# First modulation of a fused two-block network in two column halves, with the first input-projection units between them

## The chip, the cores and the metric

The kernel runs on one core of a Trainium2 chip (trn2). The metric is the device time of one execution in microseconds (us), lower is better. Before the change it is 989.19 us, the median of 3 runs from 987.23 to 992.52.

## The reference

Two transformer-like blocks on 256 tokens of width 1024, all in float32. What matters here is how the first one begins:

```python
silu_c = jax.nn.silu(c)
silu_cc = jax.nn.silu(c_ctx)
mod_l = jnp.split((silu_c @ ada_w[i] + ada_b[i])[:, None, :], 6, axis=-1)
h_l = modulate(rmsnorm(x, mix_norm_g[i]), mod_l[0], mod_l[1])      # h * (1 + scale) + shift
mod_c = jnp.split((silu_cc @ ada_w[i] + ada_b[i])[None, None, :], 6, axis=-1)
h_c = modulate(rmsnorm(xc, mix_norm_g[i]), mod_c[0], mod_c[1])
q_l, k_l, v_l, f_l = split_proj(h_l @ w_in)                        # w_in: 1024 x 2560
q_c, k_c, v_c, f_c = split_proj(h_c @ w_in)
...
```

Then come attention, a Fourier mixer, an output projection, gated feed-forward layers, a long convolution, a recurrent layer and a second attention, each a product of the 256 tokens with weights of 1024 rows or more.

## The kernel before, in words

Five engines run programs written out by hand, and wait for each other on counting semaphores. SP (the sync engine) loads the big weights, in **units** of 1 MB (128 partitions x 2048 floats, two transfers of 512 KB each) into a ring of six landing buffers `w_land`. For float32 accuracy each unit is split in two: ScalarE (ACT) writes the upper part `w_hi` (`split_hi`, L667), VectorE (DVE) writes the rest `w_lo` (`split_lo`, L1203). Both rings have three buffers. The activations are split the same way (`xT_hi`, `xT_lo`), and TensorE (PE) makes three matmuls for each product (`three`, L1950). One call of `half` (L1959) multiplies one unit with the 256 tokens: 2 token tiles x 4 row blocks x 3 matmuls of 128x512, so 24 matmuls. The two units of a 512-column chunk are its upper and its lower 512 rows; `unit_wait(u)` waits for `s_lo` (w_lo of unit u is written), and `s_used` says that a unit's buffers are free.

Ahead of unit 0 stand eight more megabytes through the same ring, which `load_unit` numbers u = -8 to -1: the columns of `ada_w` that give the first shift and scale. The first four are shift, the last four scale, each 256 rows x 1024 columns. PE multiplies them with the two condition vectors (L2060 to L2068, here called **products**, four 32-column matmuls each, 8 records in the trace), ACT copies the sums to SBUF (`ada_rows`, L791 and L793), PE adds the groups and turns them to columns (`ada0_sums`, L2054), DVE adds the bias (`mcol`, L1378) and makes the factor `a_col` (L1256, and `b_col` for the context, L1382). Only then can the tokens be scaled: x is normed (`xn`, L1252), transposed by PE (`turn_norm`, L1979), and for each of the eight row blocks DVE writes `xfull` (L1275), ACT `xT_hi` (L712) and DVE `xT_lo` (L1265).

After that, on DVE in this order: w_lo of unit 1 and 2, the statistics and norm of the context (L1248, L1252), w_lo of unit 3, the small lambda terms, `take(0)` (rotation of the first chunk's result, L1442 to L1446), w_lo of unit 4, `full_lo` for the context (`ctx_full`, L1275 and `ctxT_lo`, L1265), w_lo of unit 5, `take(1)`. On PE: chunk 0 (units 0, 1), the four small products of the Fourier matrices (L2134), the transposes of the context, chunk 1 (units 2, 3), then a wait for the last `ctx_full`, `turn_heads(0)` (transposes of the rotated result, L2096), chunk 2 (units 4, 5), `turn_heads(1)`, then chunk 2 for the context. ACT writes w_hi of a unit where its program says so; w_hi of unit 5 stands behind the eight `ctxT_hi`.

SP issues its loads in program order too, and each waits until its landing buffer is free. ACT issues small loads (rows of biases, constants), and its program goes on only when they are issued.

## Time and profile before

| what | value |
|---|---|
| median of 3 runs | 989.19 us (987.23 to 992.52) |
| the profiled execution, its own time | 991.08 us |
| span of its trace | 989.4 us |
| PE busy | 915.5 us (93%) |
| DVE busy | 740.9 us (75%) |
| ACT busy | 467.8 us (47%) |
| data moved by DMA | 229.09 MB, mean 232 GB/s |

The page of the profile gives the busy time of each engine over the span, then the span in 40 slices, the DMA queues, and the chain of work that ended last. Times inside the trace are counted from the span's start; the profiled execution's own time lies 1.7 us above its span. A row of the trace names line, engine, operation, and output and inputs; what stands in brackets is how long the engine was idle before it, and what released it. PEld is TensorE's weight load, ACTq and SPq are issues of DMAs.

### The profile page before, as it was taken

To read this page: it belongs to the slowest core of one execution; us is meant where nothing else is said; L and a number is where in the kernel's file an instruction comes from. 1 tells how busy PE (TensorE), PEld (TensorE's weight loads), DVE (VectorE), ACT (ScalarE), POOL (GpSimd) and SP (SyncE) were. 2 spreads that over 40 slices of the span, in tenths; PEclk is the share of its full clock that TensorE was granted. 3 is DMA by queue.
4 is the path that set the end of the run, shared out by engine and by line. 5 is a ranking of instruction groups with operands and counts; after the bars stand their busy time and mean duration, and the time that the engine had idled before them with its cause. 6 is when DMAs were issued, how large, how long until landed. Compare 5 with 4: busy or idle time off the path is not lost.

```text
span 989.4 us, 12483 instructions
## 1 busy us (share of the span) xinstructions
PE 915.5 (93%) x4323; PEld 718.3 (73%) x4323; DVE 740.9 (75%) x1074; ACT 467.8 (47%) x777; POOL 136.1 (14%) x204
## 2 busy tenths in 40 slices
PE   3799999899999999899978999999978998999995
PEld 0588766677888888677656688888867786777884
DVE  0598787788777768669687787677687788877574
ACT  1542247555434443453166443444336775645661
POOL 0001120404100121031001500020001020011000
PEclk8799999899999999989999999999999999999999
DMA  9987662358998888637533698898865546595001
GB/s 352 374 299 256 237 235 88 123 170 268 382 339 279 311 318 300 210 133 255 192 129 127 210 359 310 285 339 300 288 217 192 164 156 201 203 364 202 31 22 42
DMA packets 119046, 229.09 MB, mean 232 GB/s; under 512 B 8650, under 2 KB 64684, under 8 KB 119002
## 3 DMA queue, kind: packets, MB, share of 16 engines
q1 hardware_dynamic: 92608, 141.57, 41.5%
q0 software_dynamic: 24224, 86.32, 25.2%
q10 hardware_dynamic: 2170, 0.64, 0.3%
q8 instruction: 24, 0.39, 0.2%
q14 instruction: 20, 0.16, 0.0%
HBM read 227.43 MB, written 1.08 MB: 231 GB/s over the span
## 4 chain that ended last, share of the span: by engine, by line
PE 75%; DVE 13%; ACT 5%; issue 4%; DMA 2%; POOL 1%; SPq 0%; ACTq 0%; POOLq 0%; DVEq 0%
PE bank L1952 21%; PE bank L1954 20%; PE bank L1953 20%; DVE w_lo L1208 2%; DMA w_land<-ev_w_in_dram 2%; PE bank L2484 1%; DVE x L1290 1%; DVE w_lo L1321 1%; DVE tmp L1289 1%; PE bank L2325 1%; PE bank L2174 1%; PE bank L2032 1%; ACT w_hi L675 1%; DVE xT_lo L1334 1%; DMA ident<-k_ident_dram 1%
## 5 line engine op out<-in xcount | busy, mean ns | idle before, releaser
L1952 PE MATMUL bank<-w_hi,xT_hi 128*128 128x512 f32 x800 | 324.4, 406 | 21.1 <-DVE xT_lo L1334 10.3
L1954 PE MATMUL bank<-w_hi,xT_lo 128*128 128x512 f32 x800 | 314.8, 394 | 0.0
L1953 PE MATMUL bank<-w_lo,xT_hi 128*128 128x512 f32 x800 | 314.7, 393 | 0.0
L1208 DVE TENSOR_TENSOR w_lo<-w_land,w_hi 128x2048 fp32r<-128x2048 f32 x110 | 251.9, 2295 | 74.0 <-ACT w_hi L675 73.7
L675 ACT ACTIVATE w_hi<-w_land 128x2048 fp32r<-128x2048 f32 x110 | 210.3, 1915 | 117.5 <-PE bank L1954 115.1
L1952 PEld LDWEIGHTS bank<-w_hi,xT_hi 128*128 128x128 f32 x800 | 152.2, 190 | 64.1 <-issue 22.7
L1954 PEld LDWEIGHTS bank<-w_hi,xT_lo 128*128 128x128 f32 x800 | 152.0, 190 | 33.0
L1953 PEld LDWEIGHTS bank<-w_lo,xT_hi 128*128 128x128 f32 x800 | 152.4, 191 | 28.9
L1225 DVE SCALAR_TENSOR_TENSOR job_sum<-a_land,silu_c,job_sum 128x1024 f32<-128x1024 f32 x126 | 163.4, 1297 | 10.0 <-DMA a_land<-mod_w_dram 4.6
L1952 PE MATMUL bank<-w_hi,hT_hi 128*128 128x512 f32 x176 | 69.9, 397 | 2.8 <-DVE hT_lo L1579 2.8
L1954 PE MATMUL bank<-w_hi,hT_lo 128*128 128x512 f32 x176 | 68.7, 390 | 0.0
L1953 PE MATMUL bank<-w_lo,hT_hi 128*128 128x512 f32 x176 | 68.5, 389 | 0.0
L504 POOL DMA_DIRECT2D a_land<-ada_w_dram x40 | 29.3, 734 | 256.5 <-DVE job_sum L1225 256.5
L940 ACT ACTIVATE silu_g<-bank 128x256 f32<-128x256 f32 x44 | 14.5, 381 | 76.1 <-PE bank L1954 76.1
L944 ACT ACTIVATE hT_hi<-bank 128x512 fp32r<-128x512 f32 x22 | 13.2, 599 | 68.1 <-PE bank L2325 68.1
L1952 PEld LDWEIGHTS bank<-w_hi,hT_hi 128*128 128x128 f32 x176 | 33.0, 188 | 13.8 <-issue 7.3
L1954 PEld LDWEIGHTS bank<-w_hi,hT_lo 128*128 128x128 f32 x176 | 33.0, 188 | 7.1
L1953 PEld LDWEIGHTS bank<-w_lo,hT_hi 128*128 128x128 f32 x176 | 33.1, 188 | 6.5
L504 POOL DMA_DIRECT2D a_land<-mod_w_dram x24 | 17.3, 719 | 147.7 <-DVE job_sum L1225 141.9
L705 ACT ACTIVATE sq_half<-x 128x512 f32<-128x512 f32 x24 | 15.1, 630 | 44.1 <-DVE x L1290 44.1
L1575 DVE TENSOR_TENSOR hid<-silu_g,bank 128x256 f32<-128x256 f32 x44 | 16.5, 417 | 23.4 <-ACT silu_g L940 23.4
L1321 DVE TENSOR_TENSOR w_lo<-w_land,w_hi 128x1024 fp32r<-128x1024 f32 x28 | 33.7, 1217 | 0.4 <-ACT w_hi L720 0.4
(325 smaller groups left out, 1121.4 us busy)
## 6 DMA issues: line engine op xcount, KB each, us to landing
w_land<-ffn_w_dram SPq DMA_DIRECT2D x132, 512.0 KB, 5.7
a_land<-ada_w_dram POOLq DMA_DIRECT2D x40, 1024.0 KB, 6.0
a_land<-mod_w_dram POOLq DMA_DIRECT2D x24, 1024.0 KB, 5.6
w_land<-od_pw_w_dram SPq DMA_DIRECT2D x24, 512.0 KB, 4.9
w_land<-ev_w_in_dram SPq DMA_DIRECT2D x20, 512.0 KB, 11.8
w_land<-ada_w_dram SPq DMA_DIRECT2D x16, 512.0 KB, 11.3
a_land<-kv_mod_w_dram POOLq DMA_DIRECT2D x8, 1024.0 KB, 6.6
w_land<-rg_w_in_dram SPq DMA_DIRECT2D x16, 512.0 KB, 5.0
```

The source lines that it names most:

```text
L504: pool.dma_start(a_land[j % 2][:, :].rearrange("p (k n) -> p k n", k=2), kview(w)[:, 2 * j:2 * j + 2, bass.ds(col, D)]).then_inc(a_landed[ ...
L675: act.activation(w_hi[u % N_SPLIT][:, :], w_land[n % N_LAND][:, :], ACT.Copy).then_inc(s_hi, 1)
L705: act.activation(sq_half[:, n % 2, :], x[:, t, 512 * c:512 * c + 512], ACT.Square, accum_out=ss[:, 2 * t + c:2 * t + c + 1]).then_inc(sem( ...
L940: act.activation(silu_g[:, t, :], bank[t][:, 0:256], ACT.Silu).then_inc(sem("silu_g"), 1)
L944: act.activation(hT_hi[:, :, :].rearrange("p k s -> p (k s)"), bank[6][:, :], ACT.Copy).then_inc(sem("hT_hi"), 1)
L1208: dve.tensor_tensor(w_lo[u % N_SPLIT][:, :], w_land[n % N_LAND][:, :], w_hi[u % N_SPLIT][:, :].bitcast(F32), ALU.subtract).then_inc(s_lo, 1)
L1225: ins = dve.scalar_tensor_tensor(out=job_sum[:, :], in0=w, scalar=silu_c[:, c, n:n + 1], in1=job_sum[:, :], op0=ALU.mult, op1=ALU.add)
L1321: return dve.tensor_tensor(w_lo[u % N_SPLIT][:, cols], w_land[n % N_LAND][:, cols], w_hi[u % N_SPLIT][:, cols].bitcast(F32), ALU.subtract)
L1575: dve.tensor_tensor(hid[:, t, :], silu_g[:, t, :], bank[t][:, 256:512], ALU.mult).then_inc(sem("hid"), 1)
L1952: pe.matmul(dst, hi, whi, start=start, stop=False)
L1953: pe.matmul(dst, hi, wlo, start=False, stop=False)
L1954: return pe.matmul(dst, lo, whi, start=False, stop=stop)
```

## The change

The first modulation is computed in two halves of its columns: first columns 0 to 511 of shift and of scale (four units of both, `ada_half(a, 0)`), then columns 512 to 1023. SP loads the first half, x, then unit 0 and unit 2 of the old numbering (the upper 512 rows of chunks 0 and 1), then the second half, and then the rest. The new unit order is chunk 0 upper, chunk 1 upper, chunk 0 lower, chunk 1 lower (units 0, 1, 2, 3). Upper rows need only the first half of the modulation. Units 0 and 2 are split and multiplied in quarters (`x_chunk`, `x_quarter`). On PE the products of the second half stand between the matmuls of unit 1, and `turn_heads(0)` moves behind the first unit of chunk 2.

```diff
+def landing(u):
+    return u + ADA0 // 2 if u < 2 else u + ADA0
...
-HALVED = [BASE["out"] + 5, BASE["ffn0"] + 2, BASE["pw1"] + 1, BASE["pw1"] + 2, BASE["pw2"] + 5, BASE["ffn1"] + 2, BASE["rg_in"] + 1, BASE["rg_in"] + 2,
+HALVED = [0, 2, BASE["out"] + 5, BASE["ffn0"] + 2, BASE["pw1"] + 1, BASE["pw1"] + 2, BASE["pw2"] + 5, BASE["ffn1"] + 2, BASE["rg_in"] + 1, BASE["rg_in"] + 2,
...
+            def ada_half(a, h):
+                def parts(land):
+                    v = land[:, :].rearrange("p (k g n) -> p k g n", k=2, g=2)
+                    return [(v[:, :, g, :], kview(ada[0])[:, 2 * a:2 * a + 2, bass.ds(g * D + 512 * h, 512)]) for g in range(2)]
+                return parts
+            for a in range(4):
+                load_item(a, ada_half(a, 0))
             sp.dma_start(x[:, :, :], t_in["x"][0].rearrange("(t p) d -> p t d", p=P)).then_inc(sem("x_in"), 16)
+            for c in range(2):
+                load_unit(c, in_cols[c](0))
+            for a in range(4):
+                load_item(6 + a, ada_half(a, 1))
```

In ScalarE's program:

```diff
             load_rows(2)
             act.dma_start(rope[:, :, :, :], t_in["k_rope"].rearrange("(t p) c d -> p t c d", p=P)).then_inc(sem("rope_in"), 16)
+            act.wait_ge(sem("ada0_used"), ADA0 // 2)
+            act.activation(ada_rows[:, 0, :], bank[0][:, :], ACT.Copy).then_inc(sem("ada0_rows"), 1)
             act.wait_ge(sem("x_in"), 16)
             norm_square("n_x", x, xn)
...
+            split_halves(0)
+            x_hi(range(4))
+            split_hi(1)
             act.wait_ge(sem("ada0_used"), ADA0)
-            act.activation(ada_rows[:, 1, :], bank[1][:, :], ACT.Copy).then_inc(sem("ada0_rows"), 1)
-            split_hi(0)
-            split_hi(1)
-            full_hi("n_x", xfull, xT_hi)
+            act.activation(ada_rows[:, 1, :], bank[4][:, :], ACT.Copy).then_inc(sem("ada0_rows"), 1)
+            act.wait_ge(sem("four_gmm"), 1)
+            act.activation(four_g[:, :, :, :].rearrange("p c f n -> p (c f n)"), bank[4][:, :], ACT.Copy).then_inc(sem("four_gs"), 1)
+            split_halves(2)
+            x_hi(range(4, KT))
```

In VectorE's:

```diff
+            def x_quarter(k, u):
+                x_full(k)
+                x_full(k + 1)
+                split_lo_half(u, 0, half_ready(u)).then_inc(sem("w_lo_half"), 1)
+                x_low(k)
+                x_low(k + 1)
+                split_lo_half(u, 1, (s_hi, u + 1)).then_inc(s_lo, 1)
+                x_full(k + 2)
+                x_full(k + 3)
+                x_low(k + 2)
+                x_low(k + 3)
+            ada0_half(0, bank[2])
+            rows_turned(1, bank[5])
             norm_stats("n_x", x, xn)
-            rows_turned(1, bank[5])
...
+            scale_half(0)
+            x_quarter(0, 0)
             split_lo(1)
+            ada0_half(1, bank[5])
+            scale_half(1)
+            x_quarter(4, 2)
...
-            split_lo(2)
+            lambda_dots()
             norm_stats("n_ctx", ctx_x, ctx_x)
             split_lo(3)
-            lambda_dots()
             take(0)
             split_lo(4)
```

In TensorE's:

```diff
+            for a in range(4):
+                ada0_products(a)
+            ada0_sums(0, bank[2])
+            turn_rows(1, bank[5])
+            pe.wait_ge(sem("cols_in"), 2)
+            turn_norm("n_x", xn, bank[4:8])
+            def x_chunk(n, u, j):
+                pe.wait_ge(sem("w_lo_half"), n)
+                half(u, j, xT_hi, xT_lo, bank[0:2], None, "n_x", range(NT), (0, 1))
+                unit_wait(u)
+                half(u, j, xT_hi, xT_lo, bank[0:2], s_used, "n_x", range(NT), (2, 3))
+            x_chunk(1, 0, 0)
+            pe.wait_ge(*seen("full", "n_x", 4))
+            ada0_products(4)
+            pe.wait_ge(sem("ada0_cols"), 2)
+            unit_wait(1)
+            half(1, 0, xT_hi, xT_lo, bank[2:4], None, None, (0,))
+            ada0_products(5)
+            half(1, 0, xT_hi, xT_lo, bank[2:4], s_used, None, (1,))
+            ada0_products(6)
+            ada0_products(7)
+            pe.wait_ge(sem("ada0_rows"), 2)
+            ada0_sums(1, bank[5])
...
+            x_chunk(2, 2, 1)
+            pe.wait_ge(sem("four_gs"), 1)
+            pe.wait_ge(sem("cols_in"), 3)
+            turn_norm("n_ctx", ctx_x, bank[4:8])
+            unit_wait(3)
+            half(3, 1, xT_hi, xT_lo, bank[2:4], s_used)
...
+                        if (c, side, j) == (2, 0, 1):
+                            pe.wait_ge(*seen("full", "n_ctx", KT))
+                            turn_heads(0)
```

On PE, between the first matmuls of the input projection and the ones of the lower rows, the program before has nothing of the modulation; it is all ahead of unit 0 (buffer numbers: w_land_49 to 54 are the six landing buffers, w_hi_55 to 57 and w_lo_58 to 60 the two rings of three):

```order
L2066 MATMUL bank<-w_land_49,silu_pad 32x512 [waits w_landed0]
L2066 MATMUL bank<-w_land_49,silu_pad 32x512 x3
L2066 MATMUL bank<-w_land_50,silu_pad 32x512 [waits w_landed1]
L2066 MATMUL bank<-w_land_50,silu_pad 32x512 x3
L2056 MATMUL bank<-ada_sel,ada_rows 128x4 [waits ada0_rows,ada_sel]
L2056 MATMUL bank<-ada_sel,ada_rows 128x4 x3
L2056 MATMUL bank<-ada_sel,ada_rows 128x4 [waits ada0_rows]
L2056 MATMUL bank<-ada_sel,ada_rows 128x4 x3
L1952 MATMUL bank<-w_hi_55,xT_hi 128x512 [waits lo,w_lo,ada0_rows]
```

In the changed program the same engine has, from the last matmul of unit 1 to the first one of unit 2:

```order
L2021 MATMUL bank<-w_hi_56,xT_lo 128x512
L2134 MATMUL bank<-w_land_51,silu_pad 32x512 [waits w_landed2]
L2134 MATMUL bank<-w_land_51,silu_pad 32x512 x3
L2134 MATMUL bank<-w_land_52,silu_pad 32x512 [waits w_landed3]
L2134 MATMUL bank<-w_land_52,silu_pad 32x512 x3
L2123 MATMUL bank<-ada_sel,ada_rows 128x4 [waits ada0_rows]
L2123 MATMUL bank<-ada_sel,ada_rows 128x4 x3
L2117 MATMUL bank<-ident,prow 128x97 [waits prow2,ada0_cols]
L2172 MATMUL bank<-four_w,four_c 128x128 [waits consts_in]
L2172 MATMUL bank<-four_w,four_c 128x128 x3
L2019 MATMUL bank<-w_hi_57,xT_hi 128x512 [waits lo,w_lo_half]
```

So two of the products, the second sums and the Fourier products now stand between unit 1 and unit 2. ACT before, from the two copies of the sums on:

```order
L791 ACTIVATE ada_rows<-bank 128x512 [waits ada0_used]
L793 ACTIVATE ada_rows<-bank 128x512 [waits ada0_used]
L675 ACTIVATE w_hi_55<-w_land_51 128x2048 [waits w_landed2]
L675 ACTIVATE w_hi_56<-w_land_52 128x2048 [waits w_landed3]
L712 ACTIVATE xT_hi<-xfull 128x256 [waits full] x8
L675 ACTIVATE w_hi_57<-w_land_53 128x2048 [waits w_landed4]
L693 ACTIVATE ctx_junk,ss<-ctx_x 128x1024 [waits rstd,ctx_in]
L693 ACTIVATE ctx_junk,ss<-ctx_x 128x1024
```

ACT in the changed program, from the splits of unit 0 on:

```order
L743 ACTIVATE w_hi_55<-w_land_53 128x1024 [waits w_landed4] x2
L820 ACTIVATE xT_hi<-xfull 128x256 [waits full] x4
L697 ACTIVATE w_hi_56<-w_land_54 128x2048 [waits w_landed5]
L826 ACTIVATE ada_rows<-bank 128x512 [waits ada0_used]
L828 ACTIVATE four_g<-bank 128x512 [waits four_gmm]
L743 ACTIVATE w_hi_57<-w_land_53 128x1024 [waits w_landed4] x2
L820 ACTIVATE xT_hi<-xfull 128x256 [waits full] x4
L715 ACTIVATE ctx_junk,ss<-ctx_x 128x1024 [waits rstd,ctx_in]
L715 ACTIVATE ctx_junk,ss<-ctx_x 128x1024
```

The second copy of the sums and the copy of the Fourier product stand in the middle, and the split of unit 2 and the squares of the context are behind both. On PE, before `turn_heads(0)` stood between unit 3 and unit 4:

```order
L1954 MATMUL bank<-w_hi_55,xT_lo 128x512
L2096 MATMUL bank<-ident,rot 128x128 [waits rot,full]
L2096 MATMUL bank<-ident,rot 128x128 x3
L2096 MATMUL bank<-ident,rot 128x128 [waits rot]
L2096 MATMUL bank<-ident,rot 128x128 x3
L1952 MATMUL bank<-w_hi_56,xT_hi 128x512 [waits w_lo,rot]
```

Now it stands between unit 4 and unit 5:

```order
L2021 MATMUL bank<-w_hi_56,xT_lo 128x512
L2198 MATMUL bank<-ident,rot 128x128 [waits rot,full]
L2198 MATMUL bank<-ident,rot 128x128 x3
L2198 MATMUL bank<-ident,rot 128x128 [waits rot]
L2198 MATMUL bank<-ident,rot 128x128 x3
L2019 MATMUL bank<-w_hi_57,xT_hi 128x512 [waits w_lo]
```

The wait for the last `ctx_full` moves with it, from ahead of unit 4 to ahead of unit 5.

## Rows read from the trace of the kernel before

**Rows 1.** Chain of work that ended last, 15 to 90 us: start, duration, what.

```profile
39.02 0.46 DVE xfull L1275
39.48 0.33 DVE xT_lo L1265
...
49.63 1.42 DVE ctx_x L1252 x2
...
53.99 0.61 DVE rope_cos L1442
...
58.35 2.20 DVE w_lo L1208
60.55 0.47 DVE ctx_full L1275
...
66.37 1.09 PE bank L2096 x8
```

**Rows 2.** Timeline of ACT: start, duration, engine, line, operation, [idle before, releaser].

```profile
22.04 0.45 ACTq L789 DMA_DIRECT2D lam_in<-ev_lambda_k_dram  x1
...
31.31 0.60 ACT L793 ACTIVATE ada_rows<-bank 128x512 f32<-128x512 f32 x1 [8.18 <-PE bank L2066]
...
36.24 1.91 ACT L675 ACTIVATE w_hi<-w_land 128x2048 fp32r<-128x2048 f32 x1 [0.97 <-DMA w_land<-ev_w_in_dram]
...
45.58 1.04 ACT L693 ACTIVATE ctx_junk<-ctx_x 128x1024 f32<-128x1024 f32 x1
```

**Rows 3.** Timeline of DVE, the norm of x.

```profile
20.78 1.42 DVE L1252 TENSOR_SCALAR xn<-x,rstd 128x1024 f32<-128x1024 f32 x2 [0.89 <-POOL rstd L485]
```

**Rows 4.** Timeline of TensorE, 10 to 79 us: the pieces that the change moves.

```profile
10.69 5.91 PE L2066 MATMUL bank<-w_land,silu_pad 128*32 128x512 f32 x32 [0.74 <-ACT silu_pad L777]
20.45 1.94 PE L2066 MATMUL bank<-w_land,silu_pad 128*32 128x512 f32 x8 [3.85 <-DMA w_land<-ada_w_dram]
...
25.99 3.40 PE L1984 MATMUL bank<-ident,xn 128*128 128x128 f32 x16 [0.38 <-DVE pcol L1363]
29.32 1.92 PE L2066 MATMUL bank<-w_land,silu_pad 128*32 128x512 f32 x16
31.18 1.95 PE L2056 MATMUL bank<-ada_sel,ada_rows 128*128 128x4 f32 x16
39.17 0.76 PE L1952 MATMUL bank<-w_hi,xT_hi 128*128 128x512 f32 x1 [6.04 <-DVE xT_lo L1265]
...
52.24 1.08 PE L2134 MATMUL bank<-four_w,four_c 128*128 128x128 f32 x8
...
78.23 0.60 PE L2096 MATMUL bank<-ident,rot 128*128 128x128 f32 x4
```

**Rows 5.** Timeline of TensorE: matmuls at either clock, and two later pauses.

```profile
41.01 0.63 PE L1953 MATMUL bank<-w_lo,xT_hi 128*128 128x512 f32 x1
41.44 0.63 PE L1954 MATMUL bank<-w_hi,xT_lo 128*128 128x512 f32 x1
...
43.60 0.40 PE L1952 MATMUL bank<-w_hi,xT_hi 128*128 128x512 f32 x1
43.83 0.39 PE L1953 MATMUL bank<-w_lo,xT_hi 128*128 128x512 f32 x1
...
187.09 2.79 PE L2228 MATMUL bank<-ident,o_tok 128*128 128x128 f32 x12 [3.85 <-DVE o_tok L1530]
...
511.43 0.47 PE L1952 MATMUL bank<-w_hi,xT_hi 128*128 128x512 f32 x1 [3.17 <-DVE xT_lo L1746]
```

**Rows 6.** Stretches (us): busy us and instructions of PE, PEld, DVE, ACT, POOL; granted clock, DMA share, GB/s.

```profile
42.00:43.00 1.00, 1.00 (x5) 0.80 (x4) 1.00 (x4) 0.63 (x2) 0.00 (x0) 0.69 1.09 363
192.00:193.00 1.00, 1.00 (x5) 0.80 (x4) 0.85 (x4) 0.55 (x2) 1.00 (x3) 0.59 0.83 266
5.00:10.00 5.00, 0.47 (x1) 0.18 (x1) 0.18 (x2) 1.28 (x1) 0.00 (x0) 1.00 1.04 403
50.00:60.00 10.00, 10.00 (x59) 8.62 (x57) 9.79 (x19) 2.40 (x2) 1.26 (x2) 1.00 1.04 396
```

More of the change, by code:

```diff
@@ L1205, in split_lo @@
                     return
-                n = u + ADA0
+                n = landing(u)
                 dve.wait_ge(s_hi, at(u + 1, i, 6))
@@ L1380, in _ @@
[L1380 to L1385 removed]
+            bias0 = pcol[:, 0:2 * KT].rearrange("p (v h b) -> p v h b", v=2, h=2)
@@ new lines, in x_full, with x_low @@
+            def x_full(k):
+                dve.wait_ge(*seen("tr", "n_x", 4 * (k // 2) + 4))
+                dve.tensor_scalar(xfull[:, k, :], bank[4 + k // 2][:, 256 * (k % 2):256 * (k % 2) + 256], a_col[:, k:k + 1],
+                                  mc(0, k, 1), ALU.mult, ALU.add).then_inc(sem("full"), 1)
+            def x_low(k):
+                dve.wait_ge(*seen("hi", "n_x", k + 1))
+                dve.tensor_tensor(xT_lo[:, k, :], xfull[:, k, :], xT_hi[:, k, :].bitcast(F32), ALU.subtract).then_inc(sem("lo"), 1)
@@ new lines, in ada0_products @@
+            def ada0_products(a):
+                n = a if a < 4 else a + 2
+                pe.wait_ge(landed[n % N_LAND], 32 * (n // N_LAND + 1))
+                w = w_land[n % N_LAND][:, :].rearrange("p (k g n) -> p k g n", k=2, g=2)
+                for e in range(2):
+                    for g in range(2):
+                        r = 32 * (2 * e + g)
+                        ins = pe.matmul(bank[a // 4 * 4][r:r + 32, :], silu_pad[:, 2 * (a % 4) + e, :], w[:, e, g, :],
+                                        start=a % 4 == 0, stop=a % 4 == 3)
+                ins.then_inc(sem("ada0_used"), 1)
@@ new lines, in _ @@
+            turn_rows(2, bank[5])
+            pe.wait_ge(sem("consts_in"), 144)
+            for m in range(2):
+                for f in range(2):
+                    ins = pe.matmul(bank[4][:, 256 * m + P * f:256 * m + P * f + P], four_c[:, m, :], four_w[:, f, :],
+                                    start=True, stop=True)
+            ins.then_inc(sem("four_gmm"), 1)
+            x_chunk(2, 2, 1)
+            pe.wait_ge(sem("four_gs"), 1)
+            pe.wait_ge(sem("cols_in"), 3)
+            turn_norm("n_ctx", ctx_x, bank[4:8])
```

121 lines of the change are left out of this document (48 added, 73 removed).

## The prediction, as it was put on record

> **What bounds the kernel now.** I read the shares first, then the chain of work that ended last, then the timelines of the engines up to 80 us, because the change ends there. Over the whole span TensorE is busy 93% of the time, so what can be won lies where it waits. The largest such place is ahead of the first real matmul, which starts at 39.17 us after a pause of 6.04 us [rows 4]. One would think that an earlier first matmul is an earlier end. The chain says otherwise. From the landing of unit 1, which ScalarE takes up at 36.24 us [rows 2], the chain runs through VectorE: xfull and xT_lo in turn, w_lo, the norm of the context, w_lo, the rotation, w_lo, ctx_full, and only at 66.37 us does it pass to TensorE, with `turn_heads(0)` [rows 1]. TensorE meanwhile worked, but it then had to wait for the last ctx_full. Between 50 and 60 us VectorE is busy 9.79 of 10 us [rows 6]. So up to 66 us VectorE sets the time, and after it TensorE, which reaches `turn_heads(1)` at 78.23 us [rows 4]. That start is my station: behind it both programs do the same work in the same order, VectorE has slack, and what is won or lost there I carry to the end.
>
> **The change part by part, as new times of the same stations.**
>
> *First columns and x.* The products of the first half read the first four units, as before, and end at 10.69 + 5.91 = 16.60 [rows 4]. Their copy (0.60 [rows 2]) is over before x is used. The norm of x still ends at 20.78 + 1.42 = 22.20 [rows 3], since x stands in the same place of the queue. TensorE is at 1.2 GHz by then, as the 16 transposes at 25.99 were (3.40 us, 0.21 each [rows 4]); four of them give the first two row blocks at 23.2.
>
> *Unit 0.* It takes the place of the load that TensorE took up at 20.45 [rows 4], so it is there. ScalarE has issued its small loads only at 22.04 + 0.45 = 22.5 [rows 2], then splits it in two halves of 0.96 (half of 1.91 [rows 2]), to 23.45 and 24.4. VectorE: two xfull at 0.46 from 23.2 to 24.1, half a w_lo at 1.2 (half of 2.20, with its own start) to 25.3, xT_lo 0.34 to 25.7 [rows 1]. **TensorE starts the projection at about 25.9, 13.3 us earlier.** Then the two engines alternate: second xT_lo 26.0, second half of w_lo 27.2, two xfull 28.1, ScalarE's xT_hi 28.5, w_hi of unit 1 (1.91) 30.4, its w_lo (2.20) 32.6. TensorE needs 24 x 0.23 = 5.45 us for unit 0 at 2.4 GHz (0.23 from start to start at 43.60, 0.43 at 41.01 [rows 5]) and has finished with it and one product by 32.5. So unit 1 begins at 32.7, and that is VectorE and ScalarE again.
>
> *The second half of the columns.* Unit 1 costs 5.45 us, and the three products that TensorE does in and behind it 3 x 0.96 (1.92 for two at 29.32 [rows 4]), which ends at 41.0. Before, they lay in time in which it waited for data; now they lie on the path to the second columns. The last of these loads is where unit 1 was, at 36.2 [rows 2], 3.8 us before it is needed. Then copy 0.60, sums 0.98 (half of 1.95 [rows 4]), columns 0.3: 42.9, against 31.18 + 1.95 = 33.1 for all columns before. The bias transpose and Fourier products (0.2 + 1.08 [rows 4]) end at 44.2, ScalarE's copy of them at 44.8.
>
> *The rest of x.* ScalarE's halves of unit 2 stand behind that copy: 45.8 and 46.7. VectorE: half w_lo 47.0, two xT_lo 48.0, half w_lo 49.1, two xfull 50.0; ScalarE's last xT_hi 50.4. Its squares of the context, 2 x 1.04 [rows 2], are behind these: 52.5. TensorE waits from 44.2 to 47.1 and finishes unit 2 by about 55; nobody waits for that.
>
> *The old chain, later.* Statistics and GpSimd's root, 1.0 (0.89 of it the pause ahead of the norm of x [rows 3]), give 53.5, the norm 1.42 54.9 (before it ended at 49.63 + 1.42 = 51.05: **3.8 us later**), w_lo of unit 3 57.1, the rotation 58.35 - 53.99 = 4.4 to 61.5, w_lo of unit 4 63.7, ctx_full 66.33 - 60.55 = 5.8 to 69.5 [rows 1]. The lambda terms (0.8) now lie in the wait for the squares. Here the move of `turn_heads(0)` pays: unit 4 is already done. But unit 5 is not ready: its w_hi stands behind the eight ctxT_hi. 69.9, w_hi 71.8, w_lo 74.0. Its 24 matmuls end at 79.6 at full clock. **That is 1.4 us after 78.23.**
>
> *The clock.* Between the heads, over at 70.6, and unit 5 at 74.1 TensorE has nothing to do for 3.5 us. After a pause of 3.17 us a matmul took 0.47 us, its time at 2.4 GHz; after pauses of 3.85 and 6.04 us the next work ran at 1.2 GHz (transposes of 2.79 us for twelve, a first matmul of 0.76) [rows 5, 4]. The clock rose again 3.5 us after the start at 39.17 and 5.7 us after the one at 187.09: in the microseconds from 42 and from 192 it is granted 0.69 and 0.59 on the mean, so 0.5 for the first 0.6 and 0.8 of each [rows 6]. My 3.5 us lie between the two lengths, nearer to neither by much. I take the slow clock, for it fell in two of three pauses: 3.4 / 0.43 = 8 matmuls at 0.2 more, 1.6 us (2.6 at the longer rise, 0 if it stays high). The Trainium skill (TensorE: Matmul & The Clock Gate, "What's actually happening") says that the throttled state is the default and that activity releases the throttle; by that rule the idle stretch costs the 1.6 us and the median would be 992.2, by the row after 3.17 us it would cost nothing and be 990.6. The same for unit 0 costs little: if the clock rises t us after 25.9, unit 0 and a product end at 32.4 + 0.47 t, against 32.7, so 0 to 2.4 us for t up to 5.7. I take 0, since the transposes from 22.3 on are work too, and behind such transposes, which ran from 25.99, two products at 29.32 took the 1.92 us that one took before [rows 4].
>
> *Loads.* The halves are rows of 2 KB where the columns had 4 KB. Units of 2 KB rows moved 396 GB/s from 50 to 60 us, the 4 KB rows 403 from 5 to 10 [rows 6], so I cost it at nothing; unit 2 now waits for w_lo of unit 0 (27.2), with the queue filled until 36.2. In landing order it comes at about 39, the context at 42, unit 3 at 44.5, unit 4 at 47, all ahead of their use. Cover of the last product load: 3.8 us; beyond that each us costs one.
>
> **Sum:** +1.4 + 1.6 = **+3.0 us**. Against the profiled execution: span 989.4 to 992.4, its own 991.08 to 994.1. The median of the runs shown is 1.9 below that execution; 989.19 + 3.0 = **992.2 us**. The measurement tells about 0.5% (4.9 us) from no change, so this is no change that can be told, with a sign.
>
> **The rivals.**
>
> *TensorE is what bounds, and the early start comes through.* Then from 25.9 there are six units (32.7), four products (3.8), sums, Fourier products, the transposes of the context (half of 3.40) and heads (1.0 + 1.3 + 1.7 + 1.1): 67.5, 10.7 us earlier, 978.5. For it: the 6.04 us pause. Against it: behind the second columns (42.9) VectorE has 25.7 us of work of its own up to w_lo of unit 5 (a_col 0.5, half of x 3.2, unit 2 2.4, norm 1.5, lambda 0.8, three w_lo 6.6, rotation 4.4, context 6.3); even without a single wait that ends at 68.6 and unit 5 at 74.1, 4.1 us earlier, 985.1. More than 4.9 needs the second columns earlier too. 7%. Some of the waits being shorter than mine gives 0 to -4: 15%, still no change.
>
> *The slow clock decides* (the other side). If TensorE stays at 1.2 GHz through unit 0, unit 0 ends at 25.9 + 24 x 0.43 = 36.2, the product at twice its time at 38.1, and unit 1 starts 5.4 us late: 8.4 us slower, 997.6; through unit 1 also, 24 x 0.2 and 3 x 0.96 more, 16.1 us, 1005.3. For it: ahead of unit 0 TensorE has only transposes, then it waits at each pair of row blocks. Against: the products at 29.32 at the full clock, with little but transposes ahead of them. It passes the 4.9 us when the rise comes over 4.7 us after the start of unit 0 (0.47 t - 0.3 = 1.9) while unit 5 starts slow. 18%; a product load that lands over 5 us late has the same end, 3%.
>
> **How the numbers follow.** The worked chain, +1 to +4.9: 57%. Shorter waits, -4.9 to +1: 15%. Together no change within 0.5%: 72%. Faster 7%, slower 21%. The range takes the chain with the clock high at unit 5 and half of the shorter waits (-2.7, 986.5) and the chain with both longer rises (1.4 + 2.4 + 2.6 = 6.4), and 2 us, by which runs shown lie from their median: 997.5.
>
> **What would show each step.** First matmul of unit 0 near 25.9; w_lo of unit 1 over at 32.6; second mcol at 42.9; norm of the context over at 54.9; last ctx_full at 69.5 and w_lo of unit 5 at 74; second heads at 79.6 or 81.2, and the granted clock from 74 to 78. A second mcol before 40 or heads(1) before 76 would make the VectorE chain wrong; a granted clock of 0.5 beyond 31 would make the slow rival right.

## The result, and the profile after

The changed kernel takes 997.23 us (median of 7 runs, 996.36 to 999.34); the kernel before took 991.34 us in runs beside it (7 runs, 987.23 to 992.52). The ratio is 1.0062, with a 95% interval of 1.0038 to 1.0086: slower by 0.6%, a little beyond what I had called no change. The profiled executions have spans of 995.4 and 989.4 us, so +6.0 us where +3.0 was forecast.

The shares of the page say little: PE 92%, DVE 75% and ACT 47% of the span, as before within a point, and the same 229.09 MB. What changed stands in the timelines. TensorE's timeline of the changed kernel, 22 to 86 us (start, duration, engine, line, operation, idle before and releaser), against [rows 4]:

```profile
22.89 3.65 PE L2051 MATMUL bank<-ident,xn 128*128 128x128 f32 x16 [4.56 <-DVE xn L1285]
26.70 0.77 PE L2019 MATMUL bank<-w_hi,xT_hi 128*128 128x512 f32 x1 [0.16 <-DVE xT_lo L1431]
...
33.98 0.50 PE L2019 MATMUL bank<-w_hi,xT_hi 128*128 128x512 f32 x1
...
36.93 1.06 PE L2134 MATMUL bank<-w_land,silu_pad 128*32 128x512 f32 x8
...
40.88 1.93 PE L2134 MATMUL bank<-w_land,silu_pad 128*32 128x512 f32 x16
43.52 1.05 PE L2123 MATMUL bank<-ada_sel,ada_rows 128*128 128x4 f32 x8 [0.72 <-ACT ada_rows L826]
...
45.05 1.87 PE L2172 MATMUL bank<-four_w,four_c 128*128 128x128 f32 x8
50.35 0.77 PE L2019 MATMUL bank<-w_hi,xT_hi 128*128 128x512 f32 x1 [3.43 <-DVE xT_lo L1431]
...
66.46 0.47 PE L2019 MATMUL bank<-w_hi,xT_hi 128*128 128x512 f32 x1 [0.86 <-DVE w_lo L1241]
...
72.14 1.09 PE L2198 MATMUL bank<-ident,rot 128*128 128x128 f32 x8
76.71 0.80 PE L2019 MATMUL bank<-w_hi,xT_hi 128*128 128x512 f32 x1 [3.48 <-DVE w_lo L1241]
...
85.08 0.60 PE L2198 MATMUL bank<-ident,rot 128*128 128x128 f32 x4
```

The one pause of 6.04 us ahead of unit 0 is gone; the first matmul starts at 26.70 instead of 39.17. In its place stand two pauses, of 3.43 us ahead of unit 2 and of 3.48 us ahead of unit 5, and behind both the clock is low. The second heads (the start of `turn_heads(1)`) come at 85.08, 6.85 us later than before. VectorE's timeline of the same execution:

```profile
21.33 1.42 DVE L1285 TENSOR_SCALAR xn<-x,rstd 128x1024 f32<-128x1024 f32 x2 [0.90 <-POOL rstd L507]
...
44.61 0.17 DVE L1410 TENSOR_TENSOR mcol<-bank,pcol 128x8 f32<-128x8 f32 x1 [11.09 <-PE bank L2123]
...
48.53 1.23 DVE L1354 TENSOR_TENSOR w_lo<-w_land,w_hi 128x1024 fp32r<-128x1024 f32 x1 [2.25 <-ACT w_hi L743]
...
56.13 1.41 DVE L1285 TENSOR_SCALAR ctx_x<-ctx_x,rstd 128x1024 f32<-128x1024 f32 x2 [0.82 <-POOL rstd L507]
...
74.37 2.29 DVE L1241 TENSOR_TENSOR w_lo<-w_land,w_hi 128x2048 fp32r<-128x2048 f32 x1 [1.38 <-ACT w_hi L697]
```

VectorE, which had no pause left to give from 50 to 60 us, now stands idle for 11.09 us until the second sums arrive, and its whole list of later work begins behind that: the norm of the context ends at 57.54 instead of 51.05. So 6.5 of the 6.85 us stand already there. ScalarE's timeline, against [rows 2]:

```profile
42.87 0.60 ACT L826 ACTIVATE ada_rows<-bank 128x512 f32<-128x512 f32 x1 [11.68 <-PE bank L2134]
46.95 0.60 ACT L828 ACTIVATE four_g<-bank 128x512 f32<-128x512 f32 x1 [3.49 <-PE bank L2172]
47.45 1.99 ACT L743 ACTIVATE w_hi<-w_land 128x1024 fp32r<-128x1024 f32 x2
```

The split of unit 2, which needs nothing but its load, waits behind the copy of the Fourier products. The stretches give the clock (busy us and instructions of PE, PEld, DVE, ACT, POOL; granted clock, DMA share, GB/s), in order unit 0, Fourier products, unit 5:

```profile
27.00:28.00 1.00, 1.00 (x3) 0.81 (x3) 1.00 (x2) 0.00 (x0) 0.00 (x0) 0.50 0.88 283
30.00:31.00 1.00, 1.00 (x6) 0.84 (x5) 0.00 (x0) 1.00 (x1) 0.00 (x0) 1.00 1.03 398
...
45.00:47.00 2.00, 1.92 (x9) 1.62 (x9) 1.21 (x4) 0.05 (x1) 0.00 (x0) 0.54 1.05 387
76.00:82.00 6.00, 5.29 (x12) 4.13 (x13) 5.83 (x14) 2.71 (x4) 0.00 (x0) 0.50 0.53 175
```

### The profile page after: what moved, and what is told of

Its sections match the earlier page's. It is cut to its first block, busy times and chain, and to the rows that moved or that the text cites. A ratio compares the mean times of both kernels' runs of the same rounds, so it can differ in the third digit from the quotient of the medians.

```text
span 995.4 us, 12497 instructions
## 1 busy us (share of the span) xinstructions
PE 919.0 (92%) x4323; PEld 719.8 (72%) x4323; DVE 741.9 (75%) x1080; ACT 467.4 (47%) x779; POOL 136.1 (14%) x204
## 2 busy tenths in 40 slices
DMA packets 121094, 229.09 MB, mean 230 GB/s; under 512 B 8650, under 2 KB 64684, under 8 KB 121050
## 3 DMA queue, kind: packets, MB, share of 16 engines
HBM read 227.43 MB, written 1.08 MB: 230 GB/s over the span
## 4 chain that ended last, share of the span: by engine, by line
PE 75%; DVE 13%; ACT 5%; issue 4%; DMA 1%; POOL 1%; SPq 0%; POOLq 0%; ACTq 0%; DVEq 0%
PE bank L2019 21%; PE bank L2021 20%; PE bank L2020 20%; DVE w_lo L1241 2%; DVE w_lo L1354 1%; PE bank L2576 1%; DMA x<-x_dram 1%; DVE x L1323 1%; DVE tmp L1322 1%; PE bank L2417 1%; PE bank L2266 1%; PE bank L2099 1%; ACT w_hi L697 1%; PE bank L2241 1%; DVE xT_lo L1367 1%
## 5 line engine op out<-in xcount | busy, mean ns | idle before, releaser
L1241 DVE TENSOR_TENSOR w_lo<-w_land,w_hi 128x2048 fp32r<-128x2048 f32 x108 | 247.2, 2295 | 74.3 <-ACT w_hi L697 74.1
L697 ACT ACTIVATE w_hi<-w_land 128x2048 fp32r<-128x2048 f32 x108 | 206.4, 1915 | 111.7 <-PE bank L2021 111.7
L1354 DVE TENSOR_TENSOR w_lo<-w_land,w_hi 128x1024 fp32r<-128x1024 f32 x32 | 38.6, 1218 | 2.7 <-ACT w_hi L743 2.7
L743 ACT ACTIVATE w_hi<-w_land 128x1024 fp32r<-128x1024 f32 x32 | 32.4, 1049 | 3.5 <-issue 2.9
## 6 DMA issues: line engine op xcount, KB each, us to landing
w_land<-ev_w_in_dram SPq DMA_DIRECT2D x20, 512.0 KB, 10.7
```

Source lines behind the costliest of these rows:

```text
L697: act.activation(w_hi[u % N_SPLIT][:, :], w_land[n % N_LAND][:, :], ACT.Copy).then_inc(s_hi, 1)
L743: act.activation(w_hi[u % N_SPLIT][:, cols], w_land[n % N_LAND][:, cols], ACT.Copy).then_inc((sem("w_hi_half"), s_hi)[h], 1)
L1241: dve.tensor_tensor(w_lo[u % N_SPLIT][:, :], w_land[n % N_LAND][:, :], w_hi[u % N_SPLIT][:, :].bitcast(F32), ALU.subtract).then_inc(s_lo, 1)
L1354: return dve.tensor_tensor(w_lo[u % N_SPLIT][:, cols], w_land[n % N_LAND][:, cols], w_hi[u % N_SPLIT][:, cols].bitcast(F32), ALU.subtract)
```

## The experiments

"After" is the changed kernel, "station" the start of the second heads: 78.23 us before, 85.08 after. The first four ran beside one set of runs of the kernel before, then four, two and two beside others; each ratio is against its own set, whose medians lie between 989.02 and 990.58 us. Runs 1 to 3, 5, 6 and 8 have 10 executions each, run 4 has 4, run 7 has 6, runs 9 to 12 have 12.

**1. What the low clock at unit 5 costs.** Twelve matmuls whose result is thrown away fill the pause ahead of unit 5.

```diff
                             turn_heads(0)
+                            for _ in range(12):
+                                pe.matmul(bank[5][:, :], xT_hi[:, 0, 0:P], w_hi[4 % N_SPLIT][:, 0:512], start=True, stop=True)
```

> The changed kernel, plus 12 matmuls of 128x512 into an unused bank in the 3.5 us in which TensorE waits for w_lo of unit 5; they leave the computation as it is. Theory (VectorE's chain, and on top of it TensorE's clock, which falls in that pause and makes the first 14 matmuls of unit 5 slow): the clock stays high, unit 5 starts as before at 76.7 and its 24 matmuls take 5.5 us instead of 8.4; the second heads start at 82.2 instead of 85.1, the whole is 2.8 us faster than the changed kernel, span about 992.6, ratio to before 1.003. Rival (the loss sits in data that comes late, the clock only goes with it): unit 5 ends at 85 as before and the span stays 995.4.

Measured: 992.65 us, ratio 1.0023 (1.0004 to 1.0041). TensorE's timeline from 72 us:

```profile
72.19 1.09 PE L2198 MATMUL bank<-ident,rot 128*128 128x128 f32 x8
73.04 2.99 PE L2216 MATMUL bank<-w_hi,xT_hi 128*128 128x512 f32 x12
...
76.77 0.50 PE L2019 MATMUL bank<-w_hi,xT_hi 128*128 128x512 f32 x1 [0.74 <-DVE w_lo L1241]
...
82.39 0.60 PE L2198 MATMUL bank<-ident,rot 128*128 128x128 f32 x4
```

Unit 5 starts when it did, 76.77, but at 2.4 GHz, and the station comes 2.7 us earlier. So the fall of the clock costs 2.7 us there, and in this pause work that nobody needs was worth more than rest. The span fell by 5.7 us; most of the part beyond 2.7 arises from 420 us on, and is told behind run 12.

**2. The upper split of unit 5 first.** ScalarE splits unit 5 ahead of the eight `ctxT_hi`.

```diff
-                if c == 1:
-                    full_hi("n_ctx", ctx_full, ctxT_hi)
                 if c < 2:
                     split_hi(2 * c + 3)
+                if c == 1:
+                    full_hi("n_ctx", ctx_full, ctxT_hi)
```

> The changed kernel with ScalarE's w_hi of unit 5 ahead of the eight ctxT_hi instead of behind them. Theory: w_lo of unit 5 then starts right behind the last ctxT_lo at 72.9 instead of 74.4, TensorE's pause shrinks from 3.5 to 2.0 us, which is under the 3.17 us after which the clock was seen high: 1.4 from the earlier start and 2.8 from the clock, so 4.2 us, span about 991.2; if the clock falls in 2 us too, 1.4 us, span 994.0. Rival (unit 5 is bound by its load or by VectorE's order, not by ScalarE's): less than 0.5 us.

Measured: 994.52 us, ratio 1.0034 (1.0022 to 1.0047). The pause is 2.02 instead of 3.48 us, the station at 82.66. Two rows of TensorE's timeline, at its first and its fifth matmul after the pause:

```profile
75.45 0.50 PE L2019 MATMUL bank<-w_hi,xT_hi 128*128 128x512 f32 x1 [2.02 <-DVE w_lo L1241]
...
76.60 0.63 PE L2020 MATMUL bank<-w_lo,xT_hi 128*128 128x512 f32 x1
```

The unit began at 2.4 GHz and then fell to 1.2, while TensorE was at work again. A shorter pause did not save the clock. The low stretch was 7 matmuls of 0.63 us instead of 13, but the pause's length is not shown to be the reason: behind an unshortened pause of 3.48 us runs 6 and 12 had 7 slow ones too, and run 3 had 11. I had expected 4.2 us at the station, or 1.4 with the clock fallen; it was 2.4, of which 1.3 are the earlier start and the rest the shorter low stretch.

**3. The split of unit 2 ahead of the Fourier copy.**

```diff
-            act.wait_ge(sem("four_gmm"), 1)
-            act.activation(four_g...
             split_halves(2)
-            x_hi(range(4, KT))
+            x_hi(range(4, 6))
+            act.wait_ge(sem("four_gmm"), 1)
+            act.activation(four_g...
+            x_hi(range(6, KT))
```

> The changed kernel with ScalarE's copy of the Fourier product, and its wait for it, moved from ahead of the split of unit 2 to between the second and third xT_hi of the lower rows. Theory: w_hi of unit 2 starts right behind the copy of the second sums at 43.5 instead of 47.4; VectorE's first half of its w_lo at 46.3 instead of 48.5; everything up to the second heads 2.2 us earlier (82.9), span 993.2. Rival (the chain from the second columns on is bound by VectorE's own work, or by the load of unit 2): under 0.5 us, since VectorE would only wait elsewhere.

Measured: 992.87 us, ratio 1.0034 (1.0016 to 1.0051). The second columns come no earlier (44.87), but VectorE no longer waits for the split; the norm of the context begins at 53.94 instead of 56.13 and the station comes at 82.59. The order of two copies on ScalarE cost 2.2 us, but not all of it by itself: 0.8 of them are the Fourier products at the low clock, for which the split had to wait (run 4 shows the same order with these products at the high clock).

**4. The first heads back where they were**, ahead of unit 4.

```diff
-                        if (c, side, j) == (2, 0, 1):
+                        if (c, side, j) == (2, 0, 0):
                             pe.wait_ge(*seen("full", "n_ctx", KT))
                             turn_heads(0)
```

> The changed kernel with the wait for the last ctx_full and the first heads back ahead of unit 4, as before the change. Theory: TensorE stands still from 65.5 to 72.1, then heads 1.05, units 4 and 5 in 10.9 us of which 8 to 14 matmuls slow: second heads at 85.7 to 86.9, so 0.6 to 1.8 us slower than the changed kernel, since unit 5 then no longer has to wait for its w_lo (76.6). Rival (the move takes all of unit 4 off the path): 5.4 us slower, second heads at 90.5.

Measured: 997.34 us, ratio 1.0066 (1.0049 to 1.0084), station 84.78. TensorE idles 6.58 us ahead of the heads at 71.24, then runs through units 4 and 5 with four slow matmuls. The median is the changed kernel's, but the stations can't be compared as they stand, for this execution had a better start. One row of TensorE's timeline and one of VectorE's:

```profile
44.90 1.08 PE L2172 MATMUL bank<-four_w,four_c 128*128 128x128 f32 x8
...
55.20 1.42 DVE L1285 TENSOR_SCALAR ctx_x<-ctx_x,rstd 128x1024 f32<-128x1024 f32 x2 [0.82 <-POOL rstd L507]
```

Up to here the program is the changed one, and yet the Fourier products took 1.08 us instead of 1.87, and the norm of the context began at 55.20 instead of 56.13. From the norm to the station it is 29.58 us here and 28.95 in the changed kernel. So the move of the heads, which I had credited with taking unit 4 off the path, is worth about 0.6 us: nearly all that unit 4 gains, unit 5 waits for.

**5. The shape of the loads, on the kernel before.** Eight loads of the modulation in rows of 2 KB instead of 4 KB.

```diff
-                load_unit(n - ADA0, rows_pair(ada[0], n * 256))
+                load_unit(n - ADA0, cols_2k(ada[0], n * 256))
...
-                load_unit(n - ADA0, rows_pair(ada[0], (n - 4) * 256, D))
+                load_unit(n - ADA0, cols_2k(ada[0], (n - 4) * 256, D))
```

> This is the kernel before with one difference: each of the eight loads of the first modulation brings two column halves of 2 KB rows in place of one piece of 4 KB rows; order and size stay. In the changed kernel x landed at 18.04 us, before at 17.49, with nothing but that shape changed ahead of it in the queue. Theory (the shape of the loads costs the 0.55 us): x lands near 18.0 here, the second half's loads land up to another 0.5 us later, and the run is within 0.2% of the kernel before (a median 0 to 1.5 us up). Rival (0.55 us is the spread of where one profile falls, not the shape): x lands at 17.5 +/- 0.2. If the shape costs more than that, the time would go up by 2 us or more.

Measured: 989.87 us, ratio 1.0000 (0.9984 to 1.0016). ScalarE's first work on x is the landing:

```profile
18.14 1.06 ACT L700 ACTIVATE xn<-x 128x1024 f32<-128x1024 f32 x1 [7.93 <-DMA x<-x_dram]
```

In the three profiles with 4 KB rows (before, runs 10 and 11) x is there at 17.49, 17.45 and 17.64; in this one and the ten others with 2 KB rows (after, and runs 1 to 4, 6 to 9 and 12) at 17.91 to 18.39. The shape costs half a microsecond at x, and in the kernel before it is lost in TensorE's pause.

**6. The last three products ahead of unit 1's second tile.**

```diff
             ada0_products(5)
-            half(1, 0, xT_hi, xT_lo, bank[2:4], s_used, None, (1,))
             ada0_products(6)
             ada0_products(7)
+            half(1, 0, xT_hi, xT_lo, bank[2:4], None, None, (1,), (0,))
             pe.wait_ge(sem("ada0_rows"), 2)
             ada0_sums(1, bank[5])
+            half(1, 0, xT_hi, xT_lo, bank[2:4], s_used, None, (1,), (1, 2, 3))
```

> The changed kernel with the last three products (5, 6, 7) between unit 1's two token tiles and the second sums behind the first quarter of the second tile, so that the copy of the products' rows hides beside matmuls. Theory (unit 1's second tile stands ahead of the products and delays the second half of the columns by about 3 us, DVE idles 11.1 us for it): the second mcol comes at 41.7 us instead of 44.6; the Fourier products still stand behind unit 1, so their copy and the splits of unit 2 behind it on ACT come only about 1.3 us earlier; the second heads go from 85.1 to 83 to 84, the time down by 1 to 2 us. Rival (the Fourier copy ahead of unit 2's split on ACT is the whole of it): mcol earlier, unit 2 and the context's norm where they were, no change of time. Second rival: the products wait for their loads there, and unit 1 ends later: slower by 1 us or more.

Measured: 994.13 us, ratio 1.0054 (1.0032 to 1.0075), though its profiled span was 989.0. The second `mcol` comes at 41.10 instead of 44.61, and the Fourier products take 1.08 us again instead of 1.87. In this order, with matmuls of the projection between them and the four products, all four profiles have 1.08 (runs 6, 8, 9 and 12); in the order of the changed kernel five have 1.62 to 1.93 and one, run 4, has 1.08. So the order goes with the clock, but does not alone decide it. The norm of the context begins at 53.49, the station comes at 81.27. Of the 3.8 us at the station 2.6 stand at the norm, and 1.2 come from a low stretch of 7 matmuls instead of 13 at unit 5. The interval overlaps that of the unrepaired change, so only the stations speak for this edit.

**7. Unit 5 split ahead of the context on both engines, and the first heads inside it.** ScalarE as in run 2; then

```diff
+            split_lo(5)
             full_lo("n_ctx", ctx_full, ctxT_hi, ctxT_lo, bank[4:8], lambda k: b_col[:, k:k + 1],
                     lambda k: mcol_ctx[:, k:k + 1], whole=True)
-            split_lo(5)
...
-                        if (c, side, j) == (3, 0, 1):
+                        if (c, side, j) in ((2, 0, 1), (3, 0, 1)):
                             half(u, j, hi, lo, bank[b:b + 2], None, None, (0,))
-                            job_sums(0)
+                            if c == 2:
+                                pe.wait_ge(*seen("full", "n_ctx", KT))
+                                turn_heads(0)
+                            else:
+                                job_sums(0)
```

> The changed kernel with unit 5 split ahead of the context's modulation on both engines (ACT as in the run with the split moved alone, DVE's low half too), and the first heads turned between unit 5's two token tiles. Theory (moving the heads behind unit 4 was right, but unit 5's low half still stood behind the context's eight pieces on DVE, 6.7 us of work): unit 5 starts at 72.1 us right behind unit 4, at 2.4 GHz, instead of 76.7 at 1.2 GHz; the first heads come near 75 to 76, the second heads near 79 to 80 instead of 85.1; the time is 4.5 to 6 us below the changed kernel, level with the one before (ratio 0.998 to 1.003). Rival: the heads now wait inside the unit for the context's pieces (which end 2.3 us later) and the clock falls there: the second heads at 82 or later, and no more gain than the run with the split moved on ACT alone (994.5).

Measured: the station at 78.63 us, as forecast, and no gain at all: 995.53 us, ratio 1.0065 (1.0045 to 1.0086). TensorE's timeline at 125 us:

```profile
125.39 1.95 PE L2088 MATMUL bank<-ones,job_sum 128*128 128x1 f32 x16 [1.96 <-DVE job_sum L1258]
```

and VectorE's:

```profile
104.03 0.75 DVE L1255 TENSOR_SCALAR job_sum<-a_land,silu_c 128x1024 f32<-128x1024 f32 x1 [4.02 <-DMA a_land<-ada_w_dram]
```

The sums at 125.39 stood at 121.13 in the kernel before, so a lag of 1.0 us behind the heads had grown to 4.3. (The station itself lags by 0.4 only. Here its second pair of heads waits 0.2 us more for its rotation, so that in runs 7, 8, 9 and 11 the next matmul is some 0.6 us worse off than the station says.) `job_sum` is the next layer's modulation, which VectorE works off in pieces of 2.6 us between its other work; POOL loads each from HBM into one of two buffers, when the piece before has left it. The second piece began at 87.98 here, at 83.30 before. That lag of 4.7, and not the 0.4 to 1.0 us of the heads, is what arrives at the sums. It does not explain the whole median, though: at the sums the kernel is still 2.6 us ahead of the changed one (127.98), as is its profiled span (992.8), and run 1, with its sums at 125.29, has 992.65. Why the median keeps nothing of the 2.6 us stays open.

**8. The three repairs together** (3, 6 and 7).

> The three repairs in one kernel: products 5 to 7 ahead of unit 1's second tile, the Fourier copy behind unit 2's split on ACT, and unit 5 split ahead of the context's modulation with the first heads inside unit 5. Theory (each takes away its own wait of one chain: the second columns, the split behind the Fourier copy, the low half of unit 5): the context's norm begins near 51.5 to 53 us (56.1 in the changed kernel, 51.05 before), the second heads come at 75 to 77, ahead of the 78.2 of the kernel before, and the time is 2 to 4 us below the kernel before. Rival (TensorE or the loads are the bound from 45 us on, so that repairs overlap): the second heads at 79 to 80 as with the unit 5 repair alone, and the time level with before.

Measured: 990.38 us, ratio 1.0008 (0.9989 to 1.0028). TensorE's timeline:

```profile
43.34 1.08 PE L2174 MATMUL bank<-four_w,four_c 128*128 128x128 f32 x8
...
72.57 0.38 PE L2200 MATMUL bank<-ident,rot 128*128 128x128 f32 x2
...
119.33 1.95 PE L2089 MATMUL bank<-ones,job_sum 128*128 128x1 f32 x16 [1.98 <-DVE job_sum L1259]
```

The station is 5.7 us ahead of the kernel before, 12.5 ahead of the changed one, earlier than forecast, with no matmul of 128x512 at 1.2 GHz from 26.77 to that point. The next matmul is 5.0 us ahead. At 119.33 only 1.8 us are left: TensorE waited 1.16 and 1.98 us for the job's sums. So the forecast of the time, 2 to 4 us below the kernel before, failed, though its stations held.

**9. The job's second piece ahead of unit 6's low half**, in addition.

```diff
-            job_units(0, range(1))
+            job_units(0, range(2))
             split_lo(6)
             take(2)
-            job_units(0, (1,))
             split_lo(7)
```

> The kernel with the three repairs and one more edit: DVE's second piece of the modulation job (2.6 us) goes ahead of unit 6's low half and the third take, so that its landing buffer comes free, and POOL's next load starts, about 7 us earlier. With the three repairs the second heads stood 5.0 us ahead of the kernel before, but only 3.8 us were left at 100 us and 1.8 us at 121, where TensorE waited 1.2 and 2.0 us for job_sum, and DVE 4.0 us for the load of a_land. Theory (the lead was given back to the pace of those loads through two buffers): the waits before the two sums shrink to under 0.5 us, the lead at 121 us is 4 to 5 us instead of 1.8, the profiled span comes to 983 to 985 us and the median 2 to 3 us below the kernel before (ratio 0.996 to 0.998). Rival (another resource holds that point: DVE's own work or the transfers' total): the lead at 121 us stays at 2 us, and the time is level with before.

Measured: 987.10 us (983.73 to 990.19, 12 runs) beside 989.91 for the kernel before; ratio **0.9970 (0.9957 to 0.9982)**. It is faster than the kernel before and than the changed one, by little: 0.3% and 0.9% by the two ratios. TensorE's timeline:

```profile
94.09 0.64 PE L2099 MATMUL bank<-job_sum,ones 128*32 128x256 f32 x8 [0.94 <-DVE job_sum L1259]
...
117.42 1.95 PE L2088 MATMUL bank<-ones,job_sum 128*128 128x1 f32 x16
```

The sums stand 3.7 us ahead of the kernel before; there is no wait ahead of them. That is a little less than the 4 to 5 us that I expected, in part since 0.94 us are still waited ahead of the first sums.

**10. The same edit on the kernel before.**

> The kernel before with that last edit alone (the second piece of the modulation job ahead of unit 6's low half and the third take). In the kernel before the sums at 121 us waited 0.26 us at most, and unit 6's low half is not waited for. Theory (the job's pace binds only a kernel whose heads come early): no change, 0.999 to 1.001, the second heads at 78.2 and the sums at 121 +/- 0.5 us. Rival (the loads' pace binds the kernel before too): faster by 1 us or more. If unit 6's low half comes too late by the 2.6 us put ahead of it: slower by 1 to 2 us.

Measured: 990.00 us, ratio 1.0005 (0.9988 to 1.0021), the sums at 121.05. No change, as the theory said. So run 9's gain is not this edit's own.

**11. Runs 7 and 9's edits on the kernel before**, without the early start.

> The kernel before with the repairs that need no early start: unit 5 split ahead of the context's modulation on both engines, the first heads turned inside unit 5, and the job's second piece moved ahead. There is no column half here and no unit between the modulation's parts. Theory (the lead of the repaired kernel comes from the early start: in the kernel before TensorE works without a pause over 0.4 us from 39.2 to 78.2, so no reordering behind the first unit can help): no change, the second heads at 78 +/- 0.7 us, ratio 0.999 to 1.001. Rival (the order of unit 5 is what gained, and the change's early start is worth nothing): the second heads at 76 or earlier and a gain of 2 to 3 us, like the repaired kernel's.

Measured: 992.95 us, ratio 1.0041 (1.0022 to 1.0060). Slower, against both expectations. The station came at 76.61, 1.6 us earlier, and the matmul behind the heads 1.0 us earlier, which stood already at the first matmul (38.13). But VectorE's second take waited 3.57 us for the first heads, the job's third piece came to stand at 90.92 (88.58 before), and the fifth, which is loaded into the third's buffer, waited 3.94 us for its load:

```profile
102.18 0.75 DVE L1223 TENSOR_SCALAR job_sum<-a_land,silu_c 128x1024 f32<-128x1024 f32 x1 [3.94 <-DMA a_land<-ada_w_dram]
```

So the order of run 9 loses 0.4% without the early start, and with it (and its own two repairs) gains 0.3%. In this order, then, the early start is worth some microseconds; the change as made spent more than that. Which of the two edits loses here is not separated: the job's edit alone lost nothing (run 10), the order of unit 5 was not run alone on the kernel before.

**12. Repairs 3 and 6 alone**, the first heads as the change has them.

> The changed kernel with the two repairs of the second half of the modulation only (products 5 to 7 ahead of unit 1's second tile; the Fourier copy behind unit 2's split), and the first heads behind unit 4, as the change has them. Theory (the second columns and the split behind the Fourier copy cost 5.8 us of the context's chain; the wait for unit 5's low half with its fall of the clock is a second loss, which stays): the context's norm at 50.3 us (56.1 in the changed kernel), unit 5 behind a pause of 3.5 us at 70.9, the second heads at 78 to 79.5; the time level with before, ratio 0.999 to 1.001. Rival (one loss covers the other): the second heads at 82 or later, and no more gain than either repair alone (ratio 1.003).

Measured: 991.09 us, ratio 1.0016 (0.9998 to 1.0034). TensorE's timeline:

```profile
71.25 0.50 PE L2020 MATMUL bank<-w_hi,xT_hi 128*128 128x512 f32 x1 [3.48 <-DVE w_lo L1242]
...
72.06 0.50 PE L2020 MATMUL bank<-w_hi,xT_hi 128*128 128x512 f32 x1
72.36 0.63 PE L2021 MATMUL bank<-w_lo,xT_hi 128*128 128x512 f32 x1
...
78.47 0.60 PE L2200 MATMUL bank<-ident,rot 128*128 128x128 f32 x4
```

The norm of the context begins at 50.68 and the station comes at 78.47, level with before and 6.6 us earlier than in the changed kernel; the pause of 3.48 us ahead of unit 5 is still there. The gains of runs 3 and 6 at the station, 2.5 and 3.8 us, add up to it. The two waits ahead of the norm are the change's loss; with them undone the time is level within its interval.

**Later in the program.** Behind the station every kernel makes the same matmuls in the same order, and yet the lags of single profiles move, with the clock. Between 121 and 200 us the profile of the kernel before is an unlucky one: runs 5 and 10 come out 2.1 us ahead of it by 200 us, though they were 0.1 us ahead or less at 121. Part of that is the twelve transposes at 187 us, which took 2.79 us before [rows 5]; run 5 has, behind the same pause:

```profile
185.97 1.99 PE L2235 MATMUL bank<-ident,o_tok 128*128 128x128 f32 x12 [3.85 <-DVE o_tok L1537]
```

Run 8, 1.8 us ahead at 119, is 2.3 ahead at 200 us, and so level with runs 5 and 10, as its median is with the kernel before. From 420 us on the kernels differ by 1 to 3 us, again for a reason that has nothing to do with their edits. TensorE's timeline of the kernel before has this matmul behind a pause of 1.60 us:

```profile
419.26 0.77 PE L1952 MATMUL bank<-w_hi,xT_hi 128*128 128x512 f32 x1 [1.60 <-DVE xT_lo L1334]
```

That of run 1 has the same matmul behind the same pause:

```profile
422.08 0.47 PE L2019 MATMUL bank<-w_hi,xT_hi 128*128 128x512 f32 x1 [1.60 <-DVE xT_lo L1367]
```

Before, the clock stays at 0.50 for 13 matmuls there and for 8 more at 438 us; in run 1 it is 1.00 from 419 to 424. The changed kernel has the same two falls (12 and 8 matmuls, at 425 and 444 us), and run 1, without them, gains 3.2 us on it there. At 740 us every one of the kernels has a stretch of 6 to 14 slow matmuls. A single span is therefore good to some 3 us, and a station behind the last edit is the better measure of what the edit did; the median over runs is the measure of the time.

## Why the prediction was right, and where it was not

The range (986.5 to 997.5) holds 997.23, and the sign was right. That it is held is in part luck: by 0.3 us, and only with the 2 us that I had added for scatter. Of the 5.0 us between 992.2 and 997.23, 2.1 are the kernel before, whose median in the common runs was 991.34 and not 989.19; 2.9 are the change, +5.9 us where I had +3.0. Against +6.4, my chain with both longer rises of the clock, the +5.9 lies inside. The likeliest case, no change, was not what came: +0.6% lies just beyond my 0.5%. I had given 21% to slower, but for other reasons, a low clock through unit 0 or a late load of the products, and neither came. The mechanism was the one that I had worked out as the main line (57%, +1 to +4.9 us); I had its size at half. By its stations:

| station | forecast | after | lag |
|---|---|---|---|
| norm of x over | 22.20 | 22.75 | +0.5 |
| first matmul of unit 0 | 25.9 | 26.70 | +0.8 |
| unit 1 starts | 32.7 | 33.98 | +1.3 |
| second mcol | 42.9 | 44.61 | +1.7 |
| w_hi of unit 2 starts | 44.8 | 47.45 | +2.7 |
| norm of the context over | 54.9 | 57.54 | +2.6 |
| w_lo of unit 5 over | 74.0 | 76.66 | +2.7 |
| second heads | 81.2 | 85.08 | +3.9 |

- *First columns and x* was mis-sized: "x stands in the same place of the queue", but the loads ahead of it had changed shape, and x came 0.5 us later (run 5). I had costed the halves at nothing by their GB/s, 396 against 403; a latency is not read from that.
- *Unit 0*: right in kind, 12.5 us earlier instead of 13.3. ScalarE's small loads ended 0.6 us later than I took (23.1 for 22.5), and the first three matmuls ran at 1.2 GHz.
- *Second half of the columns*: the four products cost what I said (1.06 and 1.93 us), but by now they stood on the path with everything that came late ahead of them.
- *Fourier products*: taken as 1.08 us from a row at 2.4 GHz; at 1.2 GHz they took 1.87 (run 4 had 1.08, so this was not certain either). I looked for a fall of the clock in pauses, and this one came behind the products of 32 columns, with TensorE idle for no more than 0.72 us at once. The copy and the split of unit 2 stood behind them: 2.2 us by run 3, the low clock's 0.8 included.
- *The old chain, later*: right. From the norm of the context to w_lo of unit 5 I forecast 19.1 us, and it took 19.1.
- *The move of the heads* "pays": by 0.6 us at the station and by nothing in the median (run 4). In the main it moves the pause.
- *The clock at unit 5*: right that it falls, mis-sized. 1.6 us stood for 2.7 (run 1), since the low clock lasted 13 matmuls, not 8; my upper end had 2.6.
- "VectorE has slack" behind the station was true only where nothing gained; runs 7, 8 and 11 found the job's loads there, and in run 8 a lead of 5.0 us behind the heads became 1.8.
- At the station the loss was 6.85 us, at the end 6.0. Between them the rows of 187 us differ: the pause of 3.85 us is the same, but the twelve transposes behind it took 2.79 us before and 1.95 after. The edit is not the cause: run 5, which is the kernel before there, had 1.99.

```profile
193.94 1.95 PE L2320 MATMUL bank<-ident,o_tok 128*128 128x128 f32 x12 [3.85 <-DVE o_tok L1597]
```

Of the rivals, TensorE as the bound was wrong for the change as made, and half right for the repaired one (run 8: 5.7 us at the station, where that rival had 10.7). The slow clock as the decider was wrong for unit 0, where three matmuls at 0.2 more make 0.6 us. Elsewhere it weighed more than I had it: the Fourier products' 0.8 and unit 5's 2.7 us make 3.5 of the 6.85, where my line had 1.6. The page that I had weighed (the Trainium skill, TensorE: Matmul & The Clock Gate, "What's actually happening") has the throttled state as the default, released by activity. By that rule the fall at unit 5 was to be expected, and run 1 agrees: with the pause filled, unit 5 ran at 2.4 GHz. Run 12 agrees only in part: behind the same pause of 3.48 us unit 5 began at 2.4 GHz and fell behind its fourth matmul.

## What to carry to other kernels

An earlier start for one engine moves the end only if the engine behind it on the chain gets its inputs earlier too: ask what that engine now waits for (here 11.09 us), and in which order its other inputs are made. Follow a gain to the next shared buffer before counting it; here a background job with two landing buffers took back 3.2 of 5.0 us. And price work near a pause at both clocks: the same eight Fourier products took 1.08 us in one profile and 1.87 in another. Filling a pause with matmuls whose result nobody needs can be a cheap repair; in run 1 twelve of them won 2.7 us.
